# Expert stages of a two-layer mixture-of-experts step: gate and up weights requested by SyncE in halves, in an order sorted on the chip

## The reference, cut to what matters

```
probs = softmax(xt @ w_router + b_router)                 # 520 tokens x 16 experts
gidx  = group of 4 experts with the largest sum of its two best
vals, idx = top 2 within that group;  wts = vals / sum(vals)
for e in range(16):
    h = silu(xt @ w_gate[e]) * (xt @ w_up[e])             # 1024 -> 512, twice
    y = y + comb[:, e] * (h @ w_down[e])                  # 512 -> 1024
```

## Time and profile before

| what | value |
|---|---|
| time of the profiled execution | 1939.58 us |
| its span in the trace | 1936.7 us |
| median of three runs | 1937.92 us |
| TensorE busy | 1497.9 us, 77% of the span |
| VectorE, ScalarE, GpSimd busy | 775.1, 362.5, 543.3 us |
| DMA queue q0 (GpSimd), packets and bytes | 29680, 196.96 MB |
| DMA queue q1 (SyncE) | 89618, 296.38 MB |
| expert products of layer 0, from the first to the last matmul | 502.49 to 811.9 us |
| expert products of layer 1 | 1519.99 to 1871.8 us |
| TensorE idle before L1659, all of the run | 76.4 us, of it 73.6 put down to "issue" |
| TensorE idle before L1668 | 37.9 us, of it 35.7 "issue" |

### The profile page before, as it was taken

How to read it: one execution, slowest core, us unless ns; L and a number is a source line. 1 busy time by engine, 2 the same in 40 slices (tenths; PEclk the granted TensorE clock), 3 DMA queues, 4 the chain that set the end, 5 groups by cost and what they waited for, 6 DMA issues and landing times. The chain is left out here.

```text
span 1936.7 us, 23862 instructions
## 1 busy us (share of the span) xinstructions
PE 1497.9 (77%) x7886; PEld 662.9 (34%) x7887; DVE 775.1 (40%) x1374; ACT 362.5 (19%) x834; POOL 543.3 (28%) x653
## 2 busy tenths in 40 slices
PE   6899987695578978656999987777593787698845
PEld 3333335342333323213443334444241333233311
DVE  1001127566211211246955458994275311111216
ACT  1001014321111111112120113443321111011210
POOL 0000000000232433322644568770000233233421
PEclk8999998696688989877999988888795798898976
DMA  8573923545788889396879999997406177979833
GB/s 312 213 277 119 370 103 120 176 196 226 286 331 360 319 349 377 109 351 239 309 279 348 403 368 392 351 347 270 139 23 270 67 275 294 390 262 356 332 134 131
DMA packets 129337, 511.79 MB, mean 264 GB/s; under 512 B 25861, under 2 KB 47222, under 8 KB 109531
## 3 DMA queue, kind: packets, MB, share of 16 engines
q1 hardware_dynamic: 89618, 296.38, 40.8%
q0 software_dynamic: 29680, 196.96, 25.9%
q10 hardware_dynamic: 9952, 17.35, 2.7%
HBM read 622.48 MB, written 37.93 MB: 341 GB/s over the span
## 5 line engine op out<-in xcount | busy, mean ns | idle before, releaser
L1659 PE MATMUL ps<-arena_w,arena_r 128*64 128x512 f32 x992 | 250.4, 663 | 76.4 <-issue 73.6
L1766 DVE TENSOR_TENSOR arena_r<-arena_r,ps 64x512 f32<-64x512 f32 x52 | 35.9, 690 | 406.7 <-ACT arena_r L1730 406.7
L1659 PEld LDWEIGHTS ps<-arena_w,arena_r 128*64 128x64 f32 x992 | 82.0, 152 | 233.5 <-issue 233.0
L2136 POOL TENSOR_TENSOR arena_w<-arena_w,arena_r 128x1024 f32<-128x1024 f32 x55 | 129.2, 2355 | 94.0 <-DMA arena_w<-in_cache_k_dram 93.8
L2136 POOL TENSOR_TENSOR arena_r<-arena_r 128x1024 f32<-128x1024 f32 x56 | 134.4, 2403 | 41.5 <-DMA arena_r<-in_cache_k_dram 41.4
L1774 DVE SCALAR_TENSOR_TENSOR arena_r<-ps,small,arena_r 32x512 f32<-32x512 f32 x104 | 78.0, 750 | 140.5 <-ACT arena_r L1736 139.8
L1668 PE MATMUL ps<-arena_w,arena_r 128*32 128x256 f32 x1344 | 94.9, 441 | 37.9 <-issue 35.7
L2189 PE MATMUL ps<-arena_w,xt 128*128 128x512 f32 x256 | 115.6, 609 | 1.3 <-ACT xt L2365 1.3
L457 PE MATMUL ps<-arena_w,xt 128*128 128x512 f32 x256 | 113.8, 600 | 1.0 <-DVE arena_w L540 0.6
L1685 PE MATMUL ps<-arena_w,arena_r 128*64 128x512 f32 x496 | 112.8, 596 | 0.0
L1101 PE MATMUL ps<-arena_w,xt 128*128 128x512 f32 x256 | 111.4, 593 | 0.0
(11 more groups left out here) (422 smaller groups left out, 2287.5 us busy)
## 6 DMA issues: line engine op xcount, KB each, us to landing
arena_m<-in_cache_v_dram SPq DMA_DIRECT2D x120, 512.0 KB, 6.7
arena_w<-in_cache_k_dram SPq DMA_DIRECT2D x64, 512.0 KB, 8.0
arena_r<-in_cache_k_dram SPq DMA_DIRECT2D x64, 512.0 KB, 6.5
arena_w<-in_w_ada_dram SPq DMA_DIRECT2D x12, 2048.0 KB, 17.0
arena_m<-in_w_ada_dram SPq DMA_DIRECT2D x12, 2048.0 KB, 9.2
y_rows<-arena_r SPq DMA_DIRECT2D x104, 128.0 KB, 7.7
arena_w<-in_w_in_a_dram SPq DMA_DIRECT2D x6, 2048.0 KB, 13.7
arena_m<-in_w_ada_kv_dram SPq DMA_DIRECT2D x4, 2048.0 KB, 7.7
```

The costliest lines, as they stand in the source:

```text
L1659: last = nc.tensor.matmul(psg[u][TR * j:TR * (j + 1), :], xgt[:, k, lane_rows[u]], w[u][:, k, :], start=(k == 0), stop=(k == KT - 1), tile ...
L1766: V.tensor_tensor(hs[lane_rows[u], :], es[u], psg[u][TR:2 * TR, :], ALU.mult).then_inc(h_ok, 1)
L2136: G.tensor_tensor(kp[n % RING], kp[n % RING], qb[b % 2], ALU.mult).then_inc(pp_ok, 1)
```

## The change

Gate and up are no longer requested by GpSimd but by SyncE, from a table that VectorE sorts: the experts in the order of their first tile (`order`: expert, buffer offset, and the count of gate-up products after which its buffer is free). Each matrix is fetched in two halves of 1 MB, rows k = 0..3 and 4..7 of every partition (8 KB instead of 16 KB in one piece). The first halves are requested when the first half of the products of the lane's previous tile is done (`gu_half`), the second halves when all of them are (`gu_mm`). `gate_up` on TensorE waits for the first halves, multiplies k = 0..3, waits for the second halves and multiplies the rest. How many loads must have landed for a tile it reads from a second table (`needs`), which VectorE makes after its work on pair 0; TensorE waits for it (`need_ok`) ahead of pair 1. The flag of the form is read ahead of the waits. Down and the token gathers stay on GpSimd, and `col` is made after pair 0. The stores of finished rows move from SyncE to ScalarE's queue. The load of down for expert 1 waits until the first tokens are gathered.

```diff
+class ExpertWeights:
+
+    def __init__(self, nc, ctx, m, l, a):
+        self.gate_up = [[view(m.W, (2 * j + u) * 4096, KT, FF) for u in range(2)] for j in range(2)]
+        self.down = [view(m.W, (4 + u) * 4096, FF // P, D) for u in range(2)]
+        self.w_gate_up, self.w_down = (a["w_exp_gate"], a["w_exp_up"]), a["w_exp_down"]
+        self.down_rows = a["w_exp_down"].rearrange("l e (p k) n -> (l e p) (k n)", k=FF // P)
+        self.gu_in = [[ctx.enter_context(m_semaphore(nc, f"moe{l}_gu_in{h}{p}")) for p in range(2)] for h in range(2)]
+        self.wd_in = [ctx.enter_context(m_semaphore(nc, f"moe{l}_down_in{u}")) for u in range(2)]
+
+    def half(self, l, j, e, h):
+        k = KT // 2
+        return self.w_gate_up[j][l, e].rearrange("a (p k) n -> p (a k) n", k=KT)[:, k * h:k * (h + 1), :].rearrange("p k n -> p (k n)")
+
+    def first(self, sp, l, j, e):
+        for h in range(2):
+            sp.dma_start(self.gate_up[j][e][:, KT // 2 * h:KT // 2 * (h + 1), :].rearrange("p k n -> p (k n)"),
+                         self.half(l, j, slice(e, e + 1), h)).then_inc(self.gu_in[h][e], 16)
...
+            sp.wait_ge(x_in, 16)
+            weights.first_down(sp, l, 1)
+            sp.wait_ge(order_ok, 1)
+            for n in range(2, NE):
+                e = sp.value_load(order[0:1, n:n + 1], min_val=0, max_val=NE - 1)
+                lane = sp.value_load(order[0:1, NE + n:NE + n + 1], min_val=0, max_val=4096)
+                after = sp.value_load(order[0:1, 2 * NE + n:2 * NE + n + 1], min_val=1, max_val=2 * COLS)
+                for h, used in enumerate((gu_half, gu_mm)):
+                    sp.wait_ge(used, after)
+                    sp.wait_ge(gu_in[h][n % 2], 32 * (n // 2))
+                    for j in range(2):
+                        sp.dma_start(m.W[:, bass.ds(lane + 8192 * j + 2048 * h, 2048)], weights.half(l, j, bass.ds(e, 1), h)).then_inc(
+                            gu_in[h][n % 2], 16)
...
+            def load_down(i, u):
+                nc.gpsimd.tensor_copy(di[u], col[:, bass.ds(i + u * COLS, 1)]).then_inc(di_ok[u], 1)
+                g.wait_ge(di_ok[u], 2 * i - 1)
+                nc.gpsimd.tensor_tensor(d_seen[u], one, one, ALU.mult).then_inc(di_ok[u], 1)
+                g.indirect_dma_start(out=wd[u].rearrange("p k n -> p (k n)"), out_offset=None, in_=weights.down_rows,
+                                     in_offset=bass.IndirectOffsetOnAxis(ap=di[u], axis=0),
+                                     bounds_check=DEPTH * NE * P - 1, oob_is_err=False).then_inc(wd_next[u], 16)
...
             def step(i, t):
-                g.wait_ge(gu_mm, 2 * i + 1)
-                load(weights[0:2], (wg_next, wu_next), gi, g_seen, gi_ok, i + 1, 0)
                 if t != 0:
                     g.wait_ge(d_mm, 2 * i - 1)
-                    load(weights[2:3], (wd_next,), di, d_seen, di_ok, i, 0)
+                    load_down(i, 0)
                 g.wait_ge(x_tr, i + 2)
                 gather(i + 2)
-                g.wait_ge(gu_mm, 2 * i + 2)
-                load(weights[0:2], (wg_next, wu_next), gi, g_seen, gi_ok, i + 1, 1)
                 if t != 0:
                     g.wait_ge(d_mm, 2 * i)
-                    load(weights[2:3], (wd_next,), di, d_seen, di_ok, i, 1)
+                    load_down(i, 1)
...
+            def landed(i, u):
+                at = i + u * COLS
+                return [pe.value_load(needs[0:1, bass.ds(at + 2 * COLS * p, 1)], min_val=1, max_val=NE // 2) for p in range(2)]
+
+            def is_whole(i, u):
+                return pe.value_load(m.full[0:1, bass.ds(i + u * COLS, 1)], min_val=0, max_val=1)
+
+            def by_size(full, done, whole, half):
+
                 with pe.If_ne(full.val, 0):
                     whole().then_inc(done, 1)
                 with pe.Else():
@@ -1644,17 +1663,25 @@
 
             def gate_up(i, u, first):
                 n = 2 * i + u
+                full = is_whole(i, u)
+                if not first:
+                    loads = landed(i, u)
+                    pe.wait_ge(h_ok, n - 1)
                 pe.wait_ge(x_cp, i + 1)
-                if first:
-                    pe.wait_ge(wg_in[u], 16)
-                    pe.wait_ge(wu_in[u], 16)
-                else:
-                    pe.wait_ge(wg_next[u], 16 * i)
-                    pe.wait_ge(wu_next[u], 16 * i)
-                    pe.wait_ge(h_ok, n - 1)
+
+                def arrived(h):
+                    if first:
+                        pe.wait_ge(gu_in[h][u], 32)
+                    else:
+                        for p in range(2):
+                            pe.wait_ge(gu_in[h][p], loads[p] * 32)
+                arrived(0)
 
                 def whole():
                     for k in range(KT):
+                        if k == KT // 2:
+                            last.then_inc(gu_half, 1)
+                            arrived(1)
...
+            pairs = pair_count(pe)
+            step(0, 0)
+            pe.wait_ge(need_ok, 1)
+            step(1, 1)
+            with pe.Fori(2, pairs) as i:
+                step(i, None)
...
+            def y_store(i, u):
+                s.wait_ge(y_v, 2 * i + u + 1)
+                rows = m.yD[bass.ds(i * P + u * TR, TR), :]
+                for c in range(2):
+                    s.dma_start(rows[:, c * 512:(c + 1) * 512], ys[u][TR * c:TR * (c + 1), :]).then_inc(y_out[u], 16)
...
                 if t != 0:
+                    y_store(i - 1, 0)
                     y_keep(i - 1, 1, t == 1)
                 h_copy(i, t == 0)
+                if t != 0:
+                    y_store(i - 1, 1)
...
+            def load_order():
+
+                V.tensor_scalar(keys, lane, -(2.0 * TR - 1.0), None, ALU.mult)
+                v.drain()
+                V.scalar_tensor_tensor(out=keys, in0=code, scalar=2.0, in1=keys, op0=ALU.mult, op1=ALU.add)
+                V.tensor_scalar(places, lane, 4096.0, None, ALU.mult)
+                v.drain()
+                V.tensor_tensor(other, along(keys), across(keys), ALU.is_lt)
+                v.drain()
+                V.tensor_reduce(out=turn, in_=other, axis=AX.X, op=ALU.add)
+                v.drain()
+                V.tensor_tensor(hot, along(turn), across(ranks), ALU.is_equal)
+                V.tensor_scalar(keys, keys, -1.0, None, ALU.add)
+                v.drain()
+                for j, x in enumerate((ranks, places, keys)):
+                    V.tensor_tensor(other, hot, along(x), ALU.mult)
+                    v.drain()
+                    V.tensor_reduce(out=ends, in_=other, axis=AX.X, op=ALU.add)
+                    v.drain()
+                    last = V.tensor_copy(order[0:1, NE * j:NE * (j + 1)], ends[0:1])
+                last.then_inc(order_ok, 1)
...
+            def loads_needed():
+
+                V.tensor_tensor(odd, turn.unsqueeze(2).to_broadcast([P, NE, NE // 2]),
+                                odd_ranks.unsqueeze(1).to_broadcast([P, NE, NE // 2]), ALU.is_equal)
+                V.tensor_tensor(ends, code, m.route_tiles, ALU.add)
+                v.drain()
+                V.tensor_reduce(out=pair_of, in_=odd, axis=AX.X, op=ALU.add)
+                V.tensor_tensor(within, at, each(ends), ALU.is_lt)
+                v.drain()
+                V.tensor_tensor(even_need, turn, pair_of, ALU.subtract)
+                V.tensor_tensor(odd_need, turn, pair_of, ALU.add)
+                V.tensor_tensor(begun, begun, within, ALU.mult)
+                v.drain()
+                V.tensor_scalar(even_need, even_need, 0.5, 1.0, ALU.mult, ALU.add)
+                V.tensor_scalar(odd_need, odd_need, 0.5, 1.0, ALU.mult, ALU.max)
+                v.drain()
+                for p, x in enumerate((even_need, odd_need)):
+                    V.tensor_tensor(within, begun, each(x), ALU.mult)
+                    v.drain()
+                    V.tensor_reduce(out=lanes(fullf), in_=within, axis=AX.X, op=ALU.add)
+                    v.drain()
+                    last = V.tensor_scalar(needs[0:1, 2 * COLS * p:2 * COLS * (p + 1)], fullf[0:1, :], 1.0, None, ALU.max)
+                last.then_inc(need_ok, 1)
...
+            fullness()
+            load_order()
+            pairs = pair_count(v)
+            step(0, 0)
+            down_rows()
+            loads_needed()
+            step(1, 1)
+            with v.Fori(2, pairs) as i:
+                step(i, None)
```

More of the change, by code:

```diff
@@ L1197, in scalar, with first_down @@
                              bias=m.rs[0:r, 1, i:i + 1]).then_inc(self.scaled, 1)
[L1200 to L1211, removed]
+class ExpertWeights:
[13 more added lines that the diff above has]
+                         self.half(l, j, slice(e, e + 1), h)).then_inc(self.gu_in[h][e], 16)
+    def first_down(self, sp, l, e):
+        sp.dma_start(self.down[e].rearrange("p k n -> p (k n)"),
+                     self.w_down[l, e:e + 1].rearrange("a (p k) n -> p (a k n)", k=FF // P)).then_inc(self.wd_in[e], 16)
 class Router:
@@ L1252, in stage_route @@
```

(26 more changed lines are left out.)

98 lines of the change are left out of this document (52 added, 46 removed).

## The result

The changed kernel takes 1880.49 us (median; 1873.57 to 1881.87) against 1939.69 us of the kernel before on the same chip: ratio 0.9688, 95% interval 0.9657 to 0.9719. It is faster by 59 us, over twice the 28.5 us of the forecast. The profiled execution's span is 1880.0 us, against 1936.7.

What follows compares the result with a forecast made beforehand. It took late weights to bound the kernel: 155 us hang on them, the DMA engines idle for 81 us while loads are under way. 49 - 10.7 - 15.4 + 5.6 = 28.5 us won gave 1910 us, range 1880 to 1946.

Steps and rivals of the forecast that it cites:

- Products that begin at the first halves: Gate-up products on TensorE start after 2 of 4 MB, 4.9 us earlier; counted as letting gaps close, no separate gain.
- The lead itself: Gate and up requested 6.1 us earlier on average, shortening 17 DMA gaps; 49 of 81 us won after deductions.
- no lead: Rival: half a product's count comes no earlier than the whole one's, requests only 2.65 us earlier; 1937 us, chance 0.12.
- The 24 us for SyncE's issue to landing: SyncE's 1.4 us from issue to landing stays at each of 17 DMA gaps, subtracted from the 81 us.
- more closes: Rival: all 81 us of DMA gaps go and loads make up the table's wait; 1875 us, chance 0.15.
- Smaller pieces: Gate and up loads in 8 KB pieces run at 417 GB/s, 281 instead of 270.5 us: 10.7 us lost.
- The queues take turns: Rival: GpSimd's down and gather delay SyncE's halves, TensorE stops in mid-product; loss from five meetings, 1952 us with seven, chance 0.15.
- The table: TensorE waits ahead of pair 1 for VectorE's table: 2.1 us in layer 0, 13.3 in layer 1, 15.4 us lost.
- First gather: Start of each expert stage: without down of expert 1 beside it, the gather is shorter, 5.6 us won.
- Sorting: VectorE's order table adds about 6.5 us, nothing on the path; if late, up to 6.5 us.
- stores on ScalarE: Four issues of 0.47 us per pair on ScalarE, 1.9 us, hidden; without that cover 49 us.
- TensorE's reads: Two more reads per gate-up product, 0.5 us each, mostly hidden: nothing, between -24 and +12 us.

Runs made afterwards that it cites:

- e2: Changed kernel, but SyncE requests both halves only when all products of the lane's previous tile are done; products still begin at first halves: 1913.86 us.
- e3: Changed kernel with both undone: requests at the whole previous product, products only after both halves; SyncE still asks in 1 MB transfers: 1937.97 us.
- e8: As the kernel with neither lead nor early products, but one 2 MB request each for gate and up, rows of 16 KB: 1909.34 us.
- e14: Kernel with neither lead nor early products, each 1 MB half on every second partition (64), rows of 16 KB: 1914.82 us.
- e9: Kernel with neither lead nor early products, with GpSimd's down load cut into two indirect loads of 8 KB rows: 1934.26 us.
- e1: Changed kernel, but products wait for both halves of gate and up before they begin; requests still go out by halves: 1898.44 us.
- e4: Changed kernel, but down of expert 1 is requested at the start of the stage again, beside the first gather: 1886.82 us.
- e13: Kernel with neither lead nor early products, each 1 MB half on 64 adjacent partitions, rows of 16 KB: 2278.2 us.

## Why the prediction was wrong

The direction was right; the size was not. One step of the sum failed, and two others were mis-sized, in opposite directions.

*Products that begin at the first halves: failed.* "I count it as what lets the gaps close, not a second time" put them at 0. The runs give them 18 us beside the lead and 24 without it. The step took earlier requests for the only thing that closes the 81 us without DMA work. An earlier start also moves the next request: e2, with early products alone, has 21 us less DMA idle time than e3. The lead itself, 28.0 us by the sum (28.5 less the 0.5 of "no lead"), measured 33 to 40: near.

*The 24 us for SyncE's issue to landing: too much.* With whole transfers and no lead, the sum's terms give 45 - 24 - 15.4 + 5.6 = 11.2 us; e8 won 27.3 by the medians and 20.0 by the expert stages. Without the 24 it would be 35.2. The step charged the gaps with SyncE's time to landing, but GpSimd's own was already in them, and it is longer:

```profile
508.81 1.04 POOL L1583 DMA_INDIRECT arena_w<-in_w_exp_gate_dram,small  x1 [0.56 <-issue]
```

```profile
504.37 0.37 SPq L1577 DMA_DIRECT2D arena_w<-in_w_exp_gate_dram  x1
```

In stretches of 0.1 us, the idle DMA engines begin to move at 510.5 us in the kernel before, 1.7 us after that request, and at 505.3 us in e8, 0.9 us after its request. How much of the 24 this takes back, and what sorting or the stores add, the runs do not separate. The rival "more closes", 1875 us, had the time almost right, but by requests that close all of the 81 us and without the early products; 48 us of DMA idle time are left, so that its time came out near was luck.

*Smaller pieces: size wrong, in the other direction.* 10.7 us were forecast by the rate, and the rate costs about 8 (477 against 469 us busy). In the kernel after, transfers behind one another move 377 GB/s at a share of 0.93. The 341 GB/s that the Trainium skill (DMA: Bandwidth & Descriptors, Bandwidth) gives for 1 MB by itself did not apply to them. But halves cost 29 us (24.6 by the expert stages), and nothing without the down loads; that their small rows get less of the engines there fits the landings of e14 and not the time of e9, so it is not shown.

*The queues take turns: its meetings came, its price did not.* The prediction named waits of over 2 us in mid-product as a sign of being wrong, and held that five meetings would eat the gain. Seven came, 41 us together, each with a request for a down matrix in the 14 us before its end (where no new expert begins, such a request moves nothing), and the kernel is 59 us faster all the same. The waits in mid-product are not waits added: where products wait for both halves (e1), TensorE is idle for 115 us ahead of gate and up, in the kernel after for 103 in all.

*The table: confirmed.* 15.4 us forecast, with 18.1 at most; taking the wait away wins 18.0 by the expert stages and 21.6 by the medians. From the first transpose to pair 1 it is now 29.7 us in layer 0 (493.29 to 523.02) and 34.1 in layer 1 (1487.50 to 1521.55), where the earlier trace rows have 25.4 and 23.8: 4.3 and 10.2 us later, for 2.1 and 11.6 in the sum, and 1.55 us more for the clock in layer 1 (8.64 for 7.09). The later loads did not make it up.

*First gather: confirmed.* Timeline of the kernel after, answering to the earlier trace rows:

```profile
489.52 1.24 POOL L1587 DMA_INDIRECT arena_r<-xm_rows,small  x1 [0.64 <-issue]
493.29 1.94 PE L1638 MATMUL ps<-ident,arena_r 128*128 128x128 f32 x8 [5.39 <-DMA arena_r<-xm_rows,small]
...
1482.81 1.16 POOL L1587 DMA_INDIRECT arena_r<-xm_rows,small  x1 [0.57 <-issue]
...
1487.50 1.94 PE L1638 MATMUL ps<-ident,arena_r 128*128 128x128 f32 x8 [6.24 <-DMA arena_r<-xm_rows,small]
```

3.77 us instead of 7.75, and 4.69 instead of 8.48 in layer 1: 7.8 us by the trace, 5 to 6 by e4, 5.6 forecast.

*Sorting, stores on ScalarE, TensorE's reads* were put at nothing, the reads between -24 and +12. No run tests sorting or stores by themselves. Waits for ScalarE stay at 1.3 us ahead of gate and up, so the stores did not show there. Of the reads only the place was tried: reading ahead of down is 10 us slower.

Put together: 28.5 us, and 29.5 more from lead and early products (57.5 for 28.0), 16.1 more from the requests (27.3 for 11.2), 18 less from the halves (28.6 for 10.7) is 56 us; measured 59. By the expert stages the three are 57.9, 20.0 and 24.6, together 53.3. What the prediction would see as right came for the gathers (4.0 and 3.8 us sooner, for 2 to 3) and pair 1, and in part for the DMA share, 0.93 and 0.89 instead of 0.95. The idle time ahead of gate and up did not fall below 70 us: without the waits for ScalarE it is 102 us, and still 76 without the table's two waits.

## What to carry to other kernels

Earlier requests are not the only thing that closes idle time of the DMA engines: when the start of a piece of work also decides when the next load is asked for, work out both, and undo each by itself. Cutting a load in pieces had its price here beside another large load, more in when the pieces land than in GB/s, and it was nearly half of what the pieces made possible. A table that the second round waits for belongs ahead of the first round's work, where its engine would otherwise wait: moving it was worth some 20 us.

## What the runs showed of the hardware

Transfers to 64 adjacent partitions move at half the rate while the DMA engines read as fully busy, in e13:

```profile
658.00:668.00 10.00, 10.00 (x50) 3.50 (x48) 1.50 (x2) 1.39 (x3) 2.43 (x4) 1.00 0.94 208
```

208 GB/s at a share of 0.94, where whole transfers had 359 at 0.88. The same bytes on every second partition (e14) ran at 356 GB/s and 0.87. So it is the neighbourhood of the partitions (or of the rows that are read for them, which changes with it), not their number, and a busy share by itself does not say that a transfer is at full rate.

Two kernels without down loads took the same time within 0.4 us, with 2 MB and with 1 MB transfers: here the form of the transfers cost time only beside the down loads.

From the issue of a request to the first movement on idle DMA engines it was 1.7 us for GpSimd's indirect load (508.81 to 510.5 us, and 1828.85 to 1830.5, in the kernel before) and 0.9 and 1.0 us for SyncE's (504.37 to 505.3 us and 1548.44 to 1549.4 in e8).
